# 64 instead of 32 tokens taken out of the U products of a PEER layer, with GpSimd making the low parts of the odd blocks

## The reference

```python
q = (h @ w_q).reshape(b, n, 8, 256)
s1 = einsum('bnhd,kd->bnhk', q[..., :128], keys1); s2 = einsum('bnhd,kd->bnhk', q[..., 128:], keys2)
v1, i1 = top_k(s1, 16); v2, i2 = top_k(s2, 16)
top_v, top_i = top_k((v1[..., :, None] + v2[..., None, :]).reshape(b, n, 8, 256), 16)
ids = e1 * 128 + e2; wts = softmax(top_v)
act = einsum('td,tkd->tk', h, u[ids]); coef = wts * gelu(act)
out = einsum('tk,tkd->td', coef, v[ids])
```

## Time and profile before

| | us |
|---|---|
| median of 3 runs (1456.65 to 1459.38) | 1456.71 |
| the profiled execution | 1457.02 |
| its span | 1455.2 |
| TensorE busy in it | 1436.7 |

### The profile page before, as it was taken

One profiled execution on the slowest core, in us unless ns is written; L12 is line 12 of the kernel. 1 busy time (PEld: TensorE's weight loads), 2 busy tenths in 40 slices (PEclk: granted clock), 3 DMA queues, 4 the chain that ended last, 5 costly groups with the idle time before them and its releaser, 6 DMA issues.

```text
span 1455.2 us, 22338 instructions
## 1 busy us (share of the span) xinstructions
PE 1436.7 (99%) x8191; PEld 1267.2 (87%) x8191; DVE 1217.6 (84%) x2506; ACT 579.9 (40%) x877; POOL 651.9 (45%) x465
## 2 busy tenths in 40 slices
PE   8999999999999999999999999999999999999998
PEld 4888877788999999999999999888888888888886
DVE  5787868778999997999999977787787778787876
ACT  4423243622333334445554533443333333333333
POOL 0220100010579999333334343385666656665650
PEclk9999999999999999999999999999999999999999
DMA  9872433134369999799999899999999999999993
GB/s 377 295 268 87 135 112 116 44 102 158 126 219 312 319 326 329 256 360 394 385 389 381 301 349 399 383 387 402 357 360 363 373 378 367 366 371 375 367 352 137
DMA packets 164777, 432.00 MB, mean 297 GB/s; under 512 B 18656, under 2 KB 67552, under 8 KB 164704
## 3 DMA queue, kind: packets, MB, share of 16 engines
q1 hardware_dynamic: 78208, 195.54, 37.1%
q0 software_dynamic: 46656, 169.89, 31.3%
q10 hardware_dynamic: 39840, 65.71, 12.0%
HBM read 385.70 MB, written 45.37 MB: 296 GB/s over the span
## 4 chain that ended last, share of the span: by engine, by line
PE 90%; DVE 6%; DMA 2%; ACT 1%; issue 1%; SPq 0%; ACTq 0%; POOL 0%; DVEq 0%
PE ps L1908 28%; PE ps L1910 27%; PE ps L1909 27%; PE ps L2316 3%; DMA part_w<-w_ada 1%; PE ps L2254 1%; DMA ada_w<-w_ada 1%; DVE ws_lo L1231 1%; PE ps L1925 0%; DVE part_acc L1261 0%; DVE ret_rs L1520 0%; PE ps L2010 0%; PE ps L2140 0%; DVE out_tmp L1551 0%; DVE x L1585 0%
## 5 line engine op out<-in xcount | busy, mean ns | idle before, releaser
L1908 PE MATMUL ps<-hT_hi,ws_hi 128*128 128x352 f32 (+1 forms) x976 | 331.4, 340 | 1.2 <-DVE hT_lo L1238 1.0
L1909 PE MATMUL ps<-hT_lo,ws_hi 128*128 128x352 f32 (+1 forms) x976 | 326.1, 334 | 0.0
L1910 PE MATMUL ps<-hT_hi,ws_lo 128*128 128x352 f32 (+1 forms) x976 | 325.6, 334 | 0.0
L1908 PE MATMUL ps<-vs_hi,coef_hi 128*128 128x512 f32 x768 | 299.0, 389 | 1.6 <-DVE coef_lo L1865 1.6
L1909 PE MATMUL ps<-vs_lo,coef_hi 128*128 128x512 f32 x768 | 298.8, 389 | 0.0
L1910 PE MATMUL ps<-vs_hi,coef_lo 128*128 128x512 f32 x768 | 298.8, 389 | 0.0
L1106 ACT ACTIVATE vs_hi<-blk_raw 128x1024 fp32r<-128x1024 f32 x128 | 135.6, 1060 | 246.1 <-PE ps L1910 243.0
L749 POOL DMA_INDIRECT rows<-u_nat,ids x128 | 151.3, 1182 | 161.1 <-DVE sp_act L1664 138.8
L772 POOL TENSOR_TENSOR vs_lo<-blk_raw,vs_hi 128x1024 fp32r<-128x1024 f32 x60 | 144.1, 2401 | 145.5 <-DVE coef_lo L1865 145.5
L1664 DVE CUSTOM_DVE_ANT_0 rows<-rows,ps 128x1024 f32<-128x1024 f32 x160 | 190.3, 1213 | 6.8 <-DMA rows<-u_nat,ids 6.1
L1050 ACT ACTIVATE ws_hi<-blk_raw 128x1024 fp32r<-128x1024 f32 x102 | 108.0, 1059 | 212.7 <-PE ps L1910 211.3
(11 more groups left out here) (344 smaller groups left out, 2372.6 us busy)
## 6 DMA issues: line engine op xcount, KB each, us to landing
blk_raw<-u_t SPq DMA_DIRECT2D x128, 512.0 KB, 6.3
blk_raw<-v_nat SPq DMA_DIRECT2D x128, 512.0 KB, 5.3
g_dram<-g_buf ACTq DMA_DIRECT2D x124, 192.0 KB, 5.5
grp_g<-g_dram ACTq DMA_DIRECT2D x31, 768.0 KB, 7.7
w_dram<-w_stage SPq DMA_DIRECT2D x32, 512.0 KB, 9.9
grp_w<-w_dram ACTq DMA_DIRECT2D x31, 512.0 KB, 13.7
part_w<-w_ada POOLq DMA_DIRECT2D x24, 512.0 KB, 6.6
raw<-w_in SPq DMA_DIRECT2D x20, 512.0 KB, 6.4
```

What stands on the lines that cost most here:

```text
L1908: pe.matmul(o, lh, rh, start=start, stop=False, skip_group_check=True)
L1909: pe.matmul(o, lh, rl, start=False, stop=False, skip_group_check=True)
L1910: return pe.matmul(o, ll, rh, start=False, stop=stop, skip_group_check=True)
```

## The change

`FEW` becomes 64, so that `NU` is 320: 64 tokens are sparse in U, with 64 gathers instead of 32. g no longer holds ones for them: it is stored with 320 columns, and `coefficients` copies their weights instead of multiplying them. The turn of their values, four strided loads from DRAM before, is one matmul against a diagonal. Spreading begins at block 48 (`PART_A`), the 40 steps of the dense tokens end at block 92, and the eight steps of the few tokens come at blocks 113 to 120 (`FEW_AT`). The exponentials come after block 44. All four token blocks have their first-level maxima in the queries (`IN_QUERIES` = 4). `take_s` moves to ScalarE, and the low parts of the last nine query matrices to GpSimd. From block 50 on the even blocks' low parts are VectorE's, the odd ones' GpSimd's, behind the one-hots of two blocks earlier; odd blocks are rounded four ahead, into two slots of which one lies in the part of hT that belongs to the last 128 tokens. Rows are worked off on odd blocks alone. The early rows are six, two before softmax and four behind it. `V_ACT` is 62, in 42 blocks. TensorE's loops over the later U blocks are written out. Core of the diff:

```diff
-FEW = 32
+FEW = 64
-PART_A = 52
+PART_A = 48
-PART_END = PART_A + STEPS // 7 * 8 + STEPS % 7
+PART_END = PART_A + FEW_STEP // 7 * 8 + FEW_STEP % 7
+FEW_AT = 113
...
-IN_QUERIES = 3
-SEARCH_ROWS = ((0,) * 7, (0,) * 7, (2,) * 7, (1,) * 12)
-SEARCH_AT = ((14, 10), (25, 14))
-EARLY_ROWS = 10
+IN_QUERIES = 4
+POOL_QUERIES = 7
+SEARCH_ROWS = ((0,) * 7, (0,) * 7, (2,) * 6 + (1,), (2,) * 6 + (1,))
+SEARCH_AT = ((17, 13), (30, 13))
+EARLY_ROWS, EXP_ROWS = 6, 2
...
-FEW_GELU, FEW_TURN, FEW_COEF = PART_A + 34, PART_A + 38, PART_A + 47
-RES_W_AT = EB - 14
-V_ACT = 26
-V_ACT_END = 20
+FEW_GELU, FEW_TURN, FEW_COEF = FEW_AT - 4, FEW_AT - 2, FEW_AT - 1
+RES_W_AT = EB - 6
+V_ACT = 62
+V_ACT_END = 42
...
+def u_by_pool(b):
+
+    return b % 2 == 1 and REST_DVE <= b < EB - U_RING
...
-    used += [PART_A - 6] * EARLY_ROWS + [b for b in range(PART_A, EB + V_ACT_END) for _ in range(act_rows(b))]
+    used += [PART_A] * EARLY_ROWS + [b for b in range(PART_A, EB + V_ACT_END) for _ in range(act_rows(b))]
...
-        due = 13 + k if k < FIRST_ROWS else max(first[-1], used[k] - 5)
+        due = 13 + 6 * k // 5 if k < FIRST_ROWS else max(first[-1], used[k] - 5)
...
-            return b % WS_U if b < PART_A else b % 2
+            if b < PART_A:
+                return b % WS_U
+            return (0, 1, 0, WS_U)[b % 4]
+
+        def us(parts, b_slot):
+
+            if b_slot == WS_U:
+                return (hT_hi if parts is us_hi else hT_lo)[:, :, ND:N]
+            return parts[b_slot][:].rearrange("p (c n) -> p c n", c=KC)
...
+            pool.wait_ge(split_lo, 28 + POOL_QUERIES)
+            for m in range(POOL_QUERIES, 2 * PH):
+                rest_query(28 + m)
...
+            for b in range(PART_A, 2 * EB):
+                if b < EB:
+                    if b % 2 and u_by_pool(b + 2):
+                        if b < PART_END or spreads_after(b) is not None:
+                            pool.wait_ge(oh_done, max(q for q in map(spreads_after, (b - 1, b)) if q is not None) + 1)
+                        else:
+                            pool.wait_ge(*rest_of_u(b - 1))
+                        rest(b + 2)
+                    read += act_rows(b)
...
-                elif PART_A <= b and b + 2 < EB:
+                elif PART_A <= b and b % 2 == 0 and b + 2 < EB:
                     round_u(b + 2, act_done, b + 1)
                 gelu(b)
+                if PART_A - 1 <= b and b % 2 and b + 4 < EB:
+                    round_u(b + 4, act_done, b + 1)
...
-            some_rows(EARLY_ROWS)
+            some_rows(EXP_ROWS)
             dve.wait_ge(exp_done, 1)
...
             dve.tensor_copy(sp_w[:], picks[:, 2, TD, :]).then_inc(sp_w_done, 1)
+            some_rows(EARLY_ROWS - EXP_ROWS)
...
+                dve.tensor_copy(coef[:, v % 2, NU:ND], w_stage[:, 1, e, :])
...
-            def products(b, p, w, free):
-                pe.wait_ge(u_lo, b + 1)
+            def products(p, w, free, low, low_done):
+                pe.wait_ge(low, low_done)
...
+                if b == FEW_TURN:
+                    pe.wait_ge(iotas, 21)
+                    pe.wait_ge(sp_gelu, 1)
+                    pe.matmul(ps[:, 4, 0:FEW], few_diag[:], few_eye[:], start=True, stop=True).then_inc(ptr_done, 1)
+                products(b % 2, u_slot(b), b - 1, *rest_of_u(b))
```

More of the change, by code:

```diff
@@ L156, in act_rows @@
         return 0
-    if b < PART_END:
-        return 3 if spreads_after(b) is None else 1
     if b >= EB:
         return share(V_ACT, b - EB, V_ACT_END) if b < EB + V_ACT_END else 0
-    late = U_ROWS - V_ACT - FIRST_ROWS - STEPS - 3 * (PART_END - PART_A - STEPS)
-    return share(late, b - PART_END, EB - PART_END)
+    if b % 2 == 0:
+        return 0
+    if b < PART_END:
+        return 3 if spreads_after(b) is None else 2
+    if spreads_after(b) is not None:
+        return 2
+    early = sum(act_rows(i) for i in range(PART_A, PART_END)) + STEPS - FEW_STEP
+    places = [i for i in range(PART_END | 1, EB, 2) if spreads_after(i) is None]
+    return share(U_ROWS - V_ACT - FIRST_ROWS - early, places.index(b), len(places))
 def v_rows(b):
@@ L172, in mix_rows, with hi_count, u_rests @@
     return share(PICKS, b - MIX_V, EB - 4 - MIX_V) if MIX_V <= b < EB - 4 else 0
+def u_by_pool(b):
+    return b % 2 == 1 and REST_DVE <= b < EB - U_RING
+def hi_count(b):
+    return b + 1 if b < REST_DVE else b if b % 2 else b + 2
+def u_rests(b, by_pool):
+    return sum(u_by_pool(i) == by_pool for i in range(b + 1))
+U_LO, U_POOL = u_rests(EB - 1, False), u_rests(EB - 1, True)
 def pool_rest(b):
@@ L1826, in _ @@
                     dve.wait_ge(u_lo, REST_DVE)
-                if b >= REST_DVE:
+                if b >= REST_DVE and not u_by_pool(b):
                     rest_u(b)
@@ L2330, in _ @@
                 last.then_inc(ptr_done, 1)
-            products(PART_A - 1, 1, WS_U - 1, PART_A - 2)
+            products(1, WS_U - 1, PART_A - 2, u_lo, PART_A)
             def few_columns():
@@ L2337, in few_columns @@
                 last.then_inc(ptr_done, 1)
[L2339 to L2342 removed]
+            for b in range(PART_A, EB):
+                if b == FEW_TURN:
[3 more added lines that the diff above has]
+                products(b % 2, u_slot(b), b - 1, *rest_of_u(b))
+                q = spreads_after(b)
+                if q == 0:
                     pe.wait_ge(ptr_taken, 3)
[L2344 to L2346 removed]
+                if q is not None:
+                    spread(q, q % 2, 2 * q if q else None, q >= FEW_STEP)
+                if q == 0:
                     few_columns()
[L2349 to L2361 removed]
             def mix_half(p, tb, half, start, stop):
```

153 lines of the change are left out of this document (74 added, 79 removed).

## The result

The changed kernel takes 1448.72 us (median of 14 runs, 1443.08 to 1455.53) against 1459.35 us for the kernel before (14 runs, 1456.65 to 1463.95, on the same chips): a ratio of 0.9932, 95% interval 0.9915 to 0.9948, 10.6 us less. I had forecast 1432, so the change is faster, but by less than half of what I expected. The profiled execution took 1445.54 us, with a span of 1443.7. The changed kernel also scatters more: 12 us between its shortest and longest run, where before showed 7; its longest run has the lowest mean granted clock of the 14 (0.990, the others 0.991 to 0.995), and why is not shown.

What follows compares the result with a forecast made beforehand. TensorE, busy 1436.7 of 1455.2 us, was taken as the bound. The terms -41.2 + 2.1 + 1 + 10 + 1.3 + 2 = -24.8 us, from 1457.0, gave 1432 us, range 1419 to 1447.

Steps and rivals of the forecast that it cites:

- 32 columns fewer: U products: 320 columns cost 147.8 ns a matmul, over 128 blocks of 24 matmuls: -41.2 us.
- Steps with three terms, queries: Eight three-term steps instead of four +1.8 us, few tokens' values +0.3; more first-level maxima in the queries 0, bound +2.
- The search: VectorE's search beside the U products: begins about 395 us, late rows make it end near 543 us instead of 537.
- GpSimd's lead: Before spreading: GpSimd runs up to 4 or 5 us late, its lead allows about 7, TensorE does not wait; bound +5.
- The wait for softmax: Before the transposes: TensorE reaches the softmax result at about 548 us, exponentials end at about 545: +1 us.
- The first spread: One-hots ready at about 567 us behind late rows, TensorE through block 48 at 557: +10 us, bounds 0 and 16.
- the hand-over: Passage from search to spreading, where the loss was expected: +1 us at softmax, +10 us at the first one-hots.
- The spreads: In the spreading blocks VectorE needs 8.3 us a pair against TensorE's 9.0: cost 0.
- third rival: VectorE and GpSimd hold each other in the spreads, 10.7 us a pair against 9.0: about 1469 us, chance 0.05.
- End of U and V: End of U: coefficients +0.3 us, kept weights +1, bound +5. V: +2 us, bounds 0 and +12.
- second rival: DMA sets the pace in V and blocks 93 to 112, 3 to 5 us in U: 1443 to 1452 us, chance 0.11.

Runs made afterwards that it cites:

- half passes: Changed kernel with GpSimd's low parts of U blocks 4 to 47 covering half the width, so part of the U products is wrong: 1437.0 us, ratio 0.9837.
- cpf in PSUM: Changed kernel with the search's list of places in PSUM instead of SBUF, the compare table worked through in two halves: 1439.9 us, ratio 0.9863.
- the control: Kernel before the change, with only the list of places moved to PSUM and the compare in two halves: 1459.1 us, ratio 0.9997.
- busy matmuls: Changed kernel with six 512-column matmuls on an unused PSUM bank in TensorE's wait for the first one-hots: 1445.2 us, ratio 0.9903.
- three buffers: Changed kernel with three buffers instead of two for the activations of a U block: 1442.3 us, ratio 0.9892.
- best, from 48: Changed kernel, spreading from block 48, with places list in PSUM, early gathers one block apart and three activation buffers: 1429.7 us, ratio 0.9814.

## Why the prediction was wrong, point by point

The forecast held a loss of 14.4 us in the U products and the change's own parts against a gain of 41.2, and +2 in V. Measured: 33.6 against 44.2, and no more than 1 us either way in V. My absolute figure stood on 1457.0 us for the kernel before, whose median over 14 runs is 1459.35: some 2 us of the distance to 1432 are of that base, and not of the change.

*32 columns fewer: right, and too small.* -44.2 for -41.2. The pitch is 146.7 ns, not 147.8.

*Steps with three terms, queries: right.* The queries end within 0.1 us of before. The 32 added one-hot matmuls cost 1.7 us for 1.8; the turn of the few values waited 1.0 us for ScalarE, which I had at nothing.

***The search: the step that failed.*** "The search ends near 543 us instead of 537." It ended at 553.6. I had counted holds, but as lateness of GpSimd, from a row of before in which GpSimd was the one held (4.22 for 2.41 us). I took VectorE's own search time over from before, with its 6.4 us of holds, while writing that GpSimd would be "busy without a break from 420 to 550 us". GpSimd was indeed busy for 122.0 of these 130 us, but it had been for 120.5 before, so that this alone explains little. The holds went from GpSimd (8.0 us before, 3.2 now) to VectorE (6.4 before, 20.2 now), as the passes met in another order, and I had taken the order over from before. Held passes of both kinds were in the trace of before, on the search's own lines (compares of 3.28 and 4.58 us for 2.30, casts of 1.85 and 1.69 for 0.23); I had priced only GpSimd's. The half passes and cpf in PSUM show it from both sides (the search's last pass 11.9 and 9.0 us sooner), and the control shows that it costs nothing where the search has time. The Trainium skill, page "SBUF — State Buffer", section "SBUF: two separate sides", which I cited for the spreads alone, says it of any pass with two SBUF inputs (against a GpSimd pass that reads SBUF) or in a two-port mode, and for the whole length of the other's pass; the runs here agree, down to the multiply with one input in PSUM that is never held.

*GpSimd's lead: wrong too, and smaller.* "Its lead allows about 7, so TensorE does not wait for it (bound +5)." I had looked at the low parts that TensorE reads, and these were never late before block 48. But a load of U waits for a low part as well, and through the loads TensorE waited 2.2 us, inside the bound.

*The wait for softmax: +1 forecast, 7.8 measured.* It follows from the search: the softmax result came at 557.8, TensorE was there at 549.9 us (548 forecast).

*The first spread: +10 forecast, 6.3 measured, by the chain that I named.* Rows 30 and 31 waited 3.6 and 0.5 us, copies and one-hots took 6.6. Since TensorE had lost 8 us ahead of it, it asked later. The two waits together, 14.1 us, were forecast as 11: the hand-over was near in sum and wrong in its parts.

*The clock behind the waits: not in the sum.* The transposes took 0.9 us longer and the products behind them about 0.9, the first spread and what followed 2.2: 4.0 us at the 1.2 GHz level. TensorE had never waited over 1.6 us in this part before, so no row showed it, but a forecast wait of 10 us should have had a line for it. The busy matmuls show it for the second wait.

*The spreads: right.* Idle for 0.3 us between 600 and 780 (the 2.57 us that my third rival works with stands in no row; GpSimd's low part takes 2.4 there); the holding of one another that I gave 0.05 did not happen there. It happened in blocks 93 to 112, where I had looked only for the transfers: a store of g lands some 7 us after its issue, two blocks are 2 x 3.52 us, and ScalarE's buffer ring has two places. ScalarE rounds late, GpSimd's odd low part then falls on VectorE's even one (2.3 to 2.7 us for 1.22, from 793 to 834 us), and TensorE waits. 5.6 us idle up to V; three buffers leave 0.9.

*End of U and V: right.* 0.7 us of waiting for the coefficient, and no other wait in V. From 900 to 1400 us the chip moved 402 GB/s and TensorE had no idle stretch after the first block, so the second rival is out for V; late in U the price it named came (5.6 us idle, 3 to 5 forecast), by another cause.

For the U products I had forecast -26.8 and they gave -10.6. Of the 16 us between, 6.8 are softmax, 4.0 the clock, 5.9 recorded waits inside products (2.2 by late loads before block 48, 3.7 late in U), 2.1 waits for w_stage and for the few values; against them stand 3.7 at the first spread, 3.0 of pitch and 1.3 at the end of U. That is 10.8. The other 5.4 lie in small pieces: start-to-start gaps behind a wait are 0.1 to 0.3 us longer than the wait recorded, and I can't assign them further. With the holds, the pace of the rows and the store ring put right, the change does take 29 us, somewhat more than I had forecast for it as it stood.

## What to carry to other kernels

When a stage gets shorter, ask not only which engine it makes late but which *pairs* of engines meet in another order: GpSimd's passes are a tax on each VectorE pass that reads two operands from SBUF or copies within it, whenever GpSimd is the first to start, and its price is read from the passes of one line that take longer than their siblings. Put one operand of a long VectorE pass into PSUM before moving the work to another block. A ring that is as long as the latency of what it waits for is at its end (two blocks were 7.7 us and are 7.0, and a store takes 7.0); count it again at the new pace, and follow each load back to the pass that frees its buffer.

## What the runs showed of the hardware that I had not expected

- A VectorE pass that is held gets no turn between GpSimd's passes while these follow without a pause: 8.89 us for one of 0.29, behind four low parts; 4.36 for a cast of 0.23, behind two.
- The hold goes by where the operands lie: compares with cpf in SBUF 2.32 to 4.60 us, with cpf in PSUM 2 x 1.23, beside the same passes of GpSimd. A cast with its source in PSUM took 0.28 right behind one from SBUF that took 4.36.
- A wait of 6.3 us costs TensorE 2.2 more at the 1.2 GHz level, and one of 3.9 us 1.4 (best, from 48); matmuls on a spare bank that fill the wait (5.3 us of them, or 3.6) take this back in the trace; that the whole time gains by it is not shown.
- 402 GB/s were moved over 500 us with VectorE, GpSimd and TensorE all at work (and 417 in parts of it), 373 before, when no more was asked.
